# Layer 1 of a mixture-of-experts kernel: the last but one expert's down part before the last expert's up part

## The reference

```
def ec_moe(h, router, w_up, w_down):
    cap = CAPACITY_FACTOR * T // N_EXPERTS                 # 2*512/16 = 64
    aff = softmax(h @ router)
    gate, idx = top_k(swapaxes(aff, 1, 2), cap)
    xg = h[bidx, idx]
    up = einsum('becd,edf->becf', xg, w_up)                # 64x1024 @ 1024x2048
    hid = silu(up[..., :D_EXPERT]) * up[..., D_EXPERT:]
    y = einsum('becf,efd->becd', hid, w_down) * gate       # 64x1024 @ 1024x1024
    return zeros_like(h).at[bidx, idx].add(y)

x = x + g2 * ec_moe(...)        # after each layer's mixer
return rmsnorm(x, norm_final)   # after layer 1
```

## Time and profile before

| | |
|---|---|
| time, median of 3 runs | 1779.1 us (1777.41 to 1779.48) |
| time of the profiled execution | 1779.6 us |
| its span | 1777.9 us |
| TensorE clock, mean over the span | 0.983 of full |
| TensorE busy | 1644.8 us, 93% |
| VectorE / ScalarE / GpSimd busy | 710.7 / 553.4 / 182.1 us |
| bytes moved | 520.78 MB, mean 293 GB/s |

### The profile page before, as it was taken

The page is one execution under the profiler, slowest core; times in us unless marked ns, Lnnn a source line. Parts: engine busy times, 40 slices in busy tenths (PEclk is TensorE's granted clock), DMA queues, the critical chain, the costliest instruction groups (busy, mean ns, idle before and its releaser), DMA issues.

```text
span 1777.9 us, 23509 instructions
## 1 busy us (share of the span) xinstructions
PE 1644.8 (93%) x9838; PEld 879.9 (49%) x9838; DVE 710.7 (40%) x1432; ACT 553.4 (31%) x970; POOL 182.1 (10%) x203
## 2 busy tenths in 40 slices
PE   5999989879999999999989899999969998888887
PEld 3766768533333333333349788888733332222222
DVE  4567666621122122122136667766441232022223
ACT  5777883400111111111136666556310000000002
POOL 1000010010001001001011145333000000000001
PEclk8999999989999999999999999999989999999999
DMA  9554352599999999999993100012499999999996
GB/s 375 196 214 161 127 224 97 229 353 405 394 403 397 394 402 398 391 405 399 398 379 124 72 1 2 1 61 107 192 372 421 421 421 421 422 421 420 421 422 254
DMA packets 89593, 520.78 MB, mean 293 GB/s; under 512 B 11347, under 2 KB 19648, under 8 KB 33936
## 3 DMA queue, kind: packets, MB, share of 16 engines
q1 hardware_dynamic: 80128, 487.74, 67.8%
q0 software_dynamic: 9360, 31.54, 5.7%
HBM read 502.37 MB, written 16.88 MB: 292 GB/s over the span
## 4 chain that ended last, share of the span: by engine, by line
PE 58%; SPq 21%; DMA 7%; DVE 6%; ACT 6%; issue 2%; ACTq 0%; DVEq 0%; POOLq 0%
SPq L573 21%; PE wide L983 14%; PE wide L994 6%; PE wide L717 6%; PE duo L1038 6%; PE turned L647 5%; PE wide L839 4%; PE duo L1050 3%; PE duo L1268 2%; PE wide L1241 2%; DMA sb_ring_x<-ada_w 2%; DMA sb_ring_x<-moe_w_down 1%; DMA sb_ring<-ada_w 1%; ACT sb_prob L1694 1%; PE duo L1194 1%
## 5 line engine op out<-in xcount | busy, mean ns | idle before, releaser
L983 PE MATMUL wide<-sb_ring_x,sb_xT 128*64 128x512 f32 x1248 | 281.4, 596 | 17.6 <-DMA sb_ring_x<-moe_w_up 16.6
L983 PE MATMUL wide<-sb_ring,sb_xT 128*64 128x512 f32 x800 | 181.6, 597 | 13.1 <-DMA sb_ring<-moe_w_up 12.9
L983 PEld LDWEIGHTS wide<-sb_ring_x,sb_xT 128*64 128x64 f32 x1248 | 85.2, 137 | 195.2 <-issue 146.3
L1038 PE MATMUL duo<-sb_ring_x,sb_hidT 128*64 128x512 f32 x608 | 140.0, 599 | 8.8 <-DMA sb_ring_x<-moe_w_down 8.6
L2051 DVE TENSOR_TENSOR sb_hid<-wide,sb_sg 128x512 f32<-128x512 f32 x16 | 11.1, 692 | 297.5 <-ACT sb_sg_c L1511 297.5
L983 PEld LDWEIGHTS wide<-sb_ring,sb_xT 128*64 128x64 f32 x800 | 54.2, 137 | 128.9 <-issue 92.5
L1509 ACT ACTIVATE sb_sg<-wide 128x512 f32<-128x512 f32 x16 | 9.6, 597 | 324.7 <-PE wide L994 324.7
L2540 POOL TENSOR_TENSOR sb_prob<-sb_prob,sb_asum 128x768 f32<-128x768 f32 x64 | 93.9, 1467 | 154.4 <-DVE sb_asum L2349 154.4
L2051 DVE TENSOR_TENSOR sb_hid<-wide,sb_hid 128x512 f32<-128x512 f32 x16 | 11.1, 692 | 222.8 <-ACT sb_hid L1509 222.8
L1038 PEld LDWEIGHTS duo<-sb_ring_x,sb_hidT 128*64 128x64 f32 x608 | 40.3, 136 | 93.3 <-issue 72.9
L1509 ACT ACTIVATE sb_hid<-wide 128x512 f32<-128x512 f32 x16 | 9.6, 598 | 246.8 <-PE wide L983 246.8
(11 more groups left out here) (471 smaller groups left out, 2890.1 us busy)
## 6 DMA issues: line engine op xcount, KB each, us to landing
sb_ring_x<-moe_w_up SPq DMA_DIRECT2D x156, 1024.0 KB, 28.7
sb_ring<-moe_w_up SPq DMA_DIRECT2D x100, 1024.0 KB, 28.3
sb_ring_x<-moe_w_down SPq DMA_DIRECT2D x79, 1024.0 KB, 27.7
sb_ring<-moe_w_down SPq DMA_DIRECT2D x49, 1024.0 KB, 28.7
sb_ring<-ada_w SPq DMA_DIRECT2D x40, 1024.0 KB, 8.2
sb_ring<-lru_w_in SPq DMA_DIRECT2D x8, 1024.0 KB, 10.1
sb_ring_x<-ada_w SPq DMA_DIRECT2D x8, 1024.0 KB, 25.1
sb_ring<-lru_w_out SPq DMA_DIRECT2D x4, 1024.0 KB, 6.4
```

Source lines behind the costliest of these rows:

```text
L983: ins = mm(wide[n * CAPL:(n + 1) * CAPL, s, :], mine[:, k, :], w[:, at:at + BANK], start=k == 0, stop=k == KD - 1)
L1038: ins = mm(lat[n * CAPL:(n + 1) * CAPL, :], hidnT[lay][:, 2 * (c % 2) + r, h * CAPL:(h + 1) * CAPL], w[:, r, n * BANK:(n + 1) * BANK], sta ...
```

## The change

In `expert_order` and in TensorE's `experts` the down part of expert 14 and the up part of expert 15 change places, in layer 1 alone. On VectorE `output_rows(14)` changes places with `hidden(15)`. Nothing is added or removed.

```
         order = up[0] + up[1]
-        for e in range(E - 2):
+        for e in range(E - 2 - lay):
             order += down[e] + up[e + 2]
-        return order + down[E - 2] + down[E - 1]
+        if lay:
+            order += down[E - 3] + down[E - 2] + up[E - 1]
+        else:
+            order += down[E - 2]
+        return order + down[E - 1]
...
-                up(E - 1, False)
-                down(E - 2)
+                if lay == 0:
+                    up(E - 1, False)
+                    down(E - 2)
+                else:
+                    down(E - 2)
+                    up(E - 1, False)
                 turn_hid(E - 1, 2 * E if lay == 0 else E)
                 down(E - 1)
...
                     rows_lo(E // 2 - 2)
                     add_pair(E // 2 - 2)
+                    output_rows(E - 2)
                     hidden(E - 1)
-                    output_rows(E - 2)
                     output_rows(E - 1)
```

## The result

| | median, us | runs | ratio to the kernel before | 95% interval |
|---|---|---|---|---|
| before | 1779.1 | 9, 1775.95 to 1779.86 | | |
| changed | 1784.6 | 9, 1782.17 to 1789.76 | 1.0036 | 1.0027 to 1.0045 |
| changed, run again (`a_again`) beside e5 to e7 | 1782.9 (before there 1777.7) | 6 | 1.0032 | 1.0020 to 1.0043 |

The change makes the kernel slower: by the ratio 6.4 us (4.8 to 8.0) in the first series and 5.7 us (3.6 to 7.6) in the second, while the medians lie 5.5 and 5.2 us apart. One execution of e6's kernel, 1805.14 us at a mean clock of 0.932, was slow and is in no ratio. The profiled execution of the changed kernel took 1784.84 us, span 1783.1.

What follows compares the result with a forecast made beforehand. The prediction took the last transfer landing, at 1757.6 us, to set the end. Loads 0, down(14) 0, uncovered way 3.9 and clock 1.6 sum to 5.5 us, giving 1784.6 us, range 1782.0 to 1787.0.

Steps and rivals of the forecast that it cites:

- Z: End of down(15) in layer 1, 1759.58 us before; whatever moves it was to move the time by as much.
- Loads 0: Last 16 landings in layer 1: equal chunks change places, all land when they did; cost 0.
- down(14) 0: down(14) moved forward waits 1.0 us for `duo`, made good in two of four chunks; cost 0 at Z.
- The uncovered way: Path from up(15) through additions, output_rows(14), `hid`, transposes and copy to down(15), no longer beside down(14); costs 3.9 us.
- K7: Start of up(15)'s last chunk on TensorE, forecast at 1748.42 us; point from which the profiles measure to down(15).
- output_rows(14), 1.5 us of it: Two VectorE instructions ahead of `hid`, 1.53 us, counted within the 3.9 us of the uncovered way.
- The clock, 1.6 us: TensorE's 3.4 us gap before down(15)'s transposes drops the clock to 1.2 GHz; costs 1.6 us, bounds 0 and 1.9.
- The threshold: down(15) must start by 1752.48 us to keep Z; forecast to miss that by 3.9 us.
- B: Rival: the way to down(15) is uncovered but TensorE's clock stays up; 1783.0 us, chance 0.22.
- C: Rival: the last landing still sets Z because down(15) catches up; 1779.1 us, no change, chance 0.05.
- D: Rival: catching up behind down(14) fails, or the clock stays low in adding pair 7; about 1788 us, chance 0.06.
- P11: Twelfth of the last 16 chunk landings, numbered from 0, at 1747.73 us before; expected to land unchanged.

Runs made afterwards that it cites:

- e5: Kernel before with the new order of the loads alone, TensorE and VectorE orders kept; 9.4 us over the kernel before (7.1 to 11.7).
- e7: Changed kernel with 14 unread products filling TensorE's gap before turn_hid(15); 3.6 us over the kernel before (2.0 to 5.2).
- e6: Kernel before with only output_rows(14) put ahead of hidden(15) on VectorE; 2.3 us over the kernel before (0.5 to 4.1).
- e4: Changed kernel with pair 6's blocks moved from up(15) to behind down(14)'s chunks; 0.2 us over the kernel before (-1.8 to 2.0).
- e1: Changed kernel with output_rows(14) put back behind hidden(15) on VectorE; 3.4 us over the kernel before (1.6 to 5.2).
- e3: Changed kernel with output_rows(14) behind hidden(15) and 14 unread products in TensorE's gap; 2.8 us over the kernel before (0.9 to 4.6).

## Why the prediction was right

The forecast was 1784.6; the median is 1784.6. That it is the same to a tenth is luck, as the nine runs spread over 7.6 us; its terms are what the experiments bear out.

- **The end hangs on the last landing, and Z moves the time.** Right: Z over before and time over before agree in every run within the interval, from 0.0 and 0.2 (e4) to 8.4 and 9.4 (e5).
- **Loads 0, down(14) 0.** Right: in e4 both are as in the changed kernel, and it costs nothing. The wait for `duo` was 1.01 us and made good in two chunks, as forecast.
- **The uncovered way, 3.9 us.** Right: 3.9 in e7, where only the clock was held up. From K7 it was 7.94 us to down(15), and the steps of the earlier trace rows add up to 1756.36 - 1748.42 = 7.94. (Between the starts of chunks 3 and 7 the trace has five blocks of pair 6, not the six of the prediction's text; the 10.58 us are read from the rows and stand.)
- **output_rows(14), 1.5 us of it.** Right in size. But the reason given for its place was wrong. "They could have run much earlier" isn't so: `ye1` and `ye_lo` are laid out at the same address (lines 315 and 320 of the kernel before), so output_rows(14) may write only when the last block of pair 6 has read `ye_lo`. That is read from the program, not tried. By it output_rows(14) can't stand ahead of that block; it can stand behind `hid`, and there it costs nothing (e1).
- **The clock, 1.6 us.** Right in kind, too small: 2.3 and 2.8 us in two executions, above the upper bound of 1.9. The mis-sized step is how long the level stays low. I took the return from 363.77, 3.1 us after work began, and for the upper bound laid all of it into down(15); counted from the transposes, as that row has it, it would have left only 1.3 us of it there. Here the return came 5.7 us after the transposes began and 3.9 after down(15) did. Of the 2.3 us, 0.4 are in the transposes and 1.9 in down(15). The Trainium skill, "TensorE: Matmul & The Clock Gate", section "Seeing it yourself", shows a fall 5.2 us after the last matmul of its run; the traces here do not agree, with 2.3 us in the changed kernel's profile and 3.2 us in a_again's.
- **The threshold.** Right: with down(15) starting at the threshold (e4) nothing is lost. 0.9 us past it (e6) the late start costs 0.9 of the 2.2.

By the profile the sum is 3.85 + 2.29 = 6.1, against 5.5 forecast. The measured 6.4 (4.8 to 8.0) holds both. Of the rivals B fell with the clock records, C with the chain, and D's mechanisms did not occur.

## What to carry to other kernels

In a stage bound by transfers the end is the last landing plus what must follow it, and an order is judged by one number: the latest moment at which the last consumer can start and still catch up. Let the last stretch with a long way through other engines end several landings ahead of that, and put nothing in an engine's queue ahead of the one instruction on this way that could as well stand behind it. A gap on TensorE just ahead of its last burst can be paid twice, as the gap and as a burst at the lower clock: here it was with gaps of 3.46 and 2.23 us, and not with one of 1.91.

## What the runs showed that I had not expected

The moment at which the clock falls differs from case to case. Counted from the end of the last work before the gap it fell after 2.3 us in the changed kernel and after 3.2 in a_again, the same kernel with the same gap; after 3.1 in e6, where the transposes had run in between; and after 3.7 in the row at 260.6. With the gap of 1.91 us in e1 it did not fall in the one execution that was profiled; whether it stays up in every execution is not shown. It came back 5.7 and 6.7 us after work had resumed in the changed kernel and in a_again, with a pause of 0.69 us on the way, and 3.1 us after it at 363.77 before, without a pause; that the pause is the reason was not tried.

Executions of one and the same kernel lie up to 10 us apart (e3: 1778.26 to 1788.13), and the profiles show that most of such a difference comes from ahead of the stage studied here. The first product of layer 1's experts started at 1310.4 in e5's profile and at 1319.9 in e3's:

```profile
1310.42 3.65 PE L987 MATMUL wide<-sb_ring,sb_xT 128*64 128x512 f32 x16
```

```profile
1319.88 2.37 PE L987 MATMUL wide<-sb_ring,sb_xT 128*64 128x512 f32 x10
```

From that product to the landing P11 it is 432.1 us (e5) to 433.2 us (e1) in the eleven profiles, so within the stage 1 us is left of the 9.5. In the last stretch the distances repeat to some hundredths where the clock does the same: down(15) took 7.09 us in each of the six profiles in which it ran back to back with the clock up (e1 to e5 and e7). For a term of 2 us the distance between two instructions in one profile says more than ten timed runs, except where the clock has a part in it: K7 to Z differs by 0.5 us between the two profiles of the changed kernel.
